# Seven products instead of eight in the down projections of an encoder's feed-forward layers

## The reference

```python
h = rms_norm(x, ffn_norm, NORM_EPS)
gate, up = jnp.split(h @ w_gate_up, 2, axis=-1)
return x + (jax.nn.silu(gate) * up) @ w_down
```

## Time and profile before

| what | value |
|---|---|
| median of 3 runs | 1811.87 us (1810.98 to 1812.22) |
| the profiled execution | 1812.14 us, of which its span is 1810.2 us |
| TensorE busy | 1759.2 us |
| VectorE busy | 1180.5 us |
| ScalarE busy | 798.6 us |
| GpSimd busy | 275.6 us |
| granted TensorE clock, mean | 0.994 of full |

### The profile page before, as it was taken

How to read it: one execution, slowest core, us unless ns; L and a number is a source line. 1 busy time by engine, 2 the same in 40 slices (tenths; PEclk the granted TensorE clock), 3 DMA queues, 4 the chain that set the end, 5 groups by cost and what they waited for, 6 DMA issues and landing times.

```text
span 1810.2 us, 28642 instructions
## 1 busy us (share of the span) xinstructions
PE 1759.2 (97%) x11280; PEld 1552.1 (86%) x11280; DVE 1180.5 (65%) x1955; ACT 798.6 (44%) x1772; POOL 275.6 (15%) x400
## 2 busy tenths in 40 slices
PE   6999999999999999999999999999899999999998
PEld 6888777778989898989888878777799898989896
DVE  5655888787656566666556468886877474747565
ACT  5233777644433333333332348775534242424242
POOL 3201436440000000000012015362400000000000
PEclk9999999999999999999999999999999999999999
DMA  5221000202222222221222210002122222212222
GB/s 173 62 67 47 25 2 25 71 1 82 71 70 70 70 70 71 68 72 48 69 70 59 59 36 26 2 25 71 35 71 70 70 70 64 69 61 67 67 81 82
DMA packets 121732, 108.20 MB, mean 60 GB/s; under 512 B 3360, under 2 KB 95648, under 8 KB 121600
## 3 DMA queue, kind: packets, MB, share of 16 engines
q1 hardware_dynamic: 120240, 101.79, 19.0%
q0 software_dynamic: 928, 3.02, 0.6%
q10 hardware_dynamic: 432, 1.57, 0.2%
HBM read 103.22 MB, written 3.15 MB: 59 GB/s over the span
## 4 chain that ended last, share of the span: by engine, by line
PE 89%; DVE 4%; ACT 2%; POOL 2%; issue 1%; DMA 0%; ACTq 0%; POOLq 0%
PE bank L1710 16%; PE bank L1712 14%; PE bank L1711 14%; PE bank L2032 12%; PE bank L2036 12%; PE bank L2034 12%; PE bank L1804 4%; PE bank L1795 3%; PE bank L1952 1%; DVE neg_max L1387 1%; PE bank L1751 1%; POOL hrstd L620 1%; PE bank L1790 1%; ACT stage L980 1%; PE bank L1728 1%
## 5 line engine op out<-in xcount | busy, mean ns | idle before, releaser
L1710 PE MATMUL bank<-w_hi,hT_hi 128*128 128x512 f32 (+1 forms) x624 | 245.5, 393 | 9.3 <-DVE x L1496 7.2
L1712 PE MATMUL bank<-w_hi,hT_lo 128*128 128x512 f32 (+1 forms) x624 | 234.4, 376 | 0.0
L1711 PE MATMUL bank<-w_lo,hT_hi 128*128 128x512 f32 (+1 forms) x624 | 233.8, 375 | 0.0
L618 POOL TENSOR_TENSOR ms<-ss,eps_col 128x1 f32<-128x1 f32 x30 | 6.2, 208 | 1052.9 <-ACT headsq L819 1052.9
L1281 DVE TENSOR_TENSOR x<-x,bank 128x512 f32<-128x512 f32 x120 | 81.3, 687 | 118.9 <-PE bank L1712 118.4
L1710 PEld LDWEIGHTS bank<-w_hi,hT_hi 128*128 128x128 f32 x624 | 118.0, 189 | 42.7 <-DVE x L1496 10.7
L1712 PEld LDWEIGHTS bank<-w_hi,hT_lo 128*128 128x128 f32 x624 | 118.0, 189 | 21.9
L1711 PEld LDWEIGHTS bank<-w_lo,hT_hi 128*128 128x128 f32 x624 | 118.4, 190 | 17.1
L2032 PE MATMUL bank<-hT_hi,w_hi 128*128 128x384 f32 x368 | 123.5, 336 | 0.7 <-issue 0.7
L2036 PE MATMUL bank<-hT_hi,w_lo 128*128 128x384 f32 x368 | 123.6, 336 | 0.0
L2034 PE MATMUL bank<-hT_lo,w_hi 128*128 128x384 f32 x368 | 123.3, 335 | 0.0
(11 more groups left out here) (214 smaller groups left out, 4610.4 us busy)
## 6 DMA issues: line engine op xcount, KB each, us to landing
x_raw<-in_w_gate_up_dram SPq DMA_DIRECT2D x44, 512.0 KB, 5.0
w_raw<-in_w_gate_up_dram SPq DMA_DIRECT2D x44, 512.0 KB, 4.0
w_raw<-in_w_in_dram SPq DMA_DIRECT2D x36, 512.0 KB, 3.7
w_raw<-in_w_down_dram SPq DMA_DIRECT2D x36, 512.0 KB, 3.8
w_raw<-in_w_out_dram SPq DMA_DIRECT2D x16, 512.0 KB, 3.7
x_raw<-in_w_down_dram SPq DMA_DIRECT2D x8, 512.0 KB, 3.7
out_dram<-stage SPq DMA_DIRECT2D x6, 512.0 KB, 2.6
gain<-in_gains_dram POOLq DMA_DIRECT2D x4, 512.0 KB, 4.1
```

Source lines behind the costliest of these rows:

```text
L1710: pe.matmul(out, a_hi, b_hi, start=first, stop=False)
L1711: pe.matmul(out, a_hi, b_lo, start=False, stop=False)
L1712: return pe.matmul(out, a_lo, b_hi, start=False, stop=last)
```

## The change

For the four middle groups of a layer (`SEVEN`), `down_seven(g)` takes the place of `down(g)`. The result of a group is seen as 2 x 2 blocks: two halves of the tokens (384 rows) by two halves of the columns (512); the inner dimension as two pairs of D_FF tiles. With A the activations and B the weights of the group:

| product | token part | weights | added to block of x |
|---|---|---|---|
| 0 | A11 | B11 | 11 |
| 1 | S1 = A21 + A22 | T1 = B12 - B11 | 22 |
| 2 | S2 = S1 - A11 | T2 = B22 - T1 | 12 (with product 0) |
| 3 | S4 = A12 - S2 | B22 | 12 (with product 1) |
| 4 | S3 = A11 - A21 | T3 = B22 - B12 | 22 (with 0 and 2) |
| 5 | A12 | B21 | 11 |
| 6 | A22 | T4 = B21 - T2 | 21 (with 0, 2 and 4) |

Each product is 2 inner tiles x 3 token tiles x 3 matmuls of 512 columns, and VectorE adds its three banks to x behind it. Even products use banks 6, 7 and 5, odd ones 2, 3 and 4. The token parts are split into halves in two places (`part_hi`, `part_lo`, 768 columns each), and the weights pass through the ring as before, 14 operands instead of 8. S1 and T1 to T4 (1024 columns each) are made by VectorE, the other token sums by GpSimd. B22 and B21 are loaded into the tile `gain` (a fifth raw buffer), B11 and B12 into the two w_raw. Tiles of these groups have no `act_high` and `act_low`; `gated` writes `act_raw` instead. In the tile that follows such a group the two w_raw buffers change places, and its first combinations are made two operands later.

The core of the diff, VectorE's list first:

```diff
@@ vector, stage of the next group's first tile @@
                     up_second(l, j - 1)
                     operand_low(l, s + 6)
+                    g = group_before(j)
+                    if g in SEVEN:
+                        operand_low(l, s + 7)
+                        operand_low(l, s + 8)
+                        down_combination(l, g, T1)
+                        gate_first(l, j)
+                        part_low(l, g, 0)
+                        operand_low(l, s + 9)
+                        operand_low(l, s + 10)
+                        down_combination(l, g, T2)
+                        up_first(l, j - 1)
+                        gated(l, j - 1)
+                        sum_first(l, g)
+                        operand_low(l, s + 11)
+                        part_low(l, g, 1)
+                        down_combination(l, g, T3)
+                        for i in range(12, 15):
+                            operand_low(l, s + i)
+                        for i in range(1, 6):
+                            add_seven(l, g, i - 1, 0)
+                            part_low(l, g, i + 1)
+                            add_seven(l, g, i - 1, 1)
+                            operand_low(l, s + (13 + 2 * i))
+                            add_seven(l, g, i - 1, 2)
+                            operand_low(l, s + (14 + 2 * i))
+                            if i == 2:
+                                down_combination(l, g, T4)
+                        for i in (5, 6):
+                            for m in range(3):
+                                add_seven(l, g, i, m)
+                        continue
@@ scalar @@
+                    if g in SEVEN:
+                        operand_high(l, s + 8)
+                        part_high(l, g, 0)
+                        silu_first(l, j)
+                        operand_high(l, s + 9)
+                        operand_high(l, s + 10)
+                        silu_second(l, j - 1)
+                        operand_high(l, s + 11)
+                        part_high(l, g, 1)
+                        for i in range(12, 15):
+                            operand_high(l, s + i)
+                        for i in range(1, 6):
+                            operand_high(l, s + (13 + 2 * i))
+                            part_high(l, g, i + 1)
+                            operand_high(l, s + (14 + 2 * i))
+                        operand_high(l, s + 25)
+                        continue
@@ gpsimd @@
+            def later_sum(l, g, n):
+                e = SEVEN.index(g)
+                if n == 0:
+                    pool.wait_ge(first_sum.sem, first_sum.at(l, e))
+                    out, a, b = act_quarter(1, 0), act_quarter(0, 0), act_quarter(1, 0)
+                elif n == 1:
+                    pool.wait_ge(part_lo_done.sem, part_lo_done.at(l, 7 * e))
+                    pool.wait_ge(later_sums.sem, later_sums.at(l, 3 * e))
+                    out, a, b = act_quarter(0, 0), act_sum[:, :, :], act_quarter(0, 0)
+                else:
+                    pool.wait_ge(part_lo_done.sem, part_lo_done.at(l, 7 * e + 1))
+                    pool.wait_ge(later_sums.sem, later_sums.at(l, 3 * e + 1))
+                    out, a, b = act_sum[:, :, :], act_quarter(0, 1), act_quarter(0, 0)
+                pool.tensor_tensor(out, a, b, ALU.subtract).then_inc(later_sums.sem, 1)
...
-                pool.wait_ge(h_ready.sem, h_ready.at(l, 2 * T - 1))
-
+                for g in SEVEN:
+                    later_sum(l, g, 0)
+                    later_sum(l, g, 1)
+                    later_sum(l, g, 2)
+
+                pool.wait_ge(ff_lo.sem, ff_lo.at(l, seven_operand(SEVEN[-1], 6, 1)))
                 pool.dma_start(gain[:, :],
@@ tensor @@
+                def down_seven(g):
+                    j = FIRST[g] + 3
+                    for i in range(7):
+                        pe.wait_ge(part_lo_done.sem, part_lo_done.at(l, 7 * SEVEN.index(g) + i))
+                        for k in range(2):
+                            r = seven_operand(g, i, k)
+                            b_hi, b_lo = ring_of(r)
+                            pe.wait_ge(ff_lo.sem, ff_lo.at(l, r))
+                            for m in range(3):
+                                b = (DOWN_W if i % 2 else DOWN_X)[m]
+                                if k == 0:
+                                    if i >= 2:
+                                        pe.wait_ge(x_added.sem, x_added.at(l, seven_added(g, i - 2, m)))
...
+                                pe.matmul(o, a_hi, b_hi, start=begin, stop=False, skip_group_check=True)
+                                pe.matmul(o, a_hi, b_lo, start=False, stop=False, skip_group_check=True)
+                                last = pe.matmul(o, a_lo, b_hi, start=False, stop=k == 1, skip_group_check=True)
@@ sync, load_seven @@
+                for b, kk, c in ((B22, 2, 1), (B11, 0, 0), (B12, 0, 1), (B21, 2, 0)):
...
+                    elif b == B11:
+                        sp.wait_ge(ff_lo.sem, ff_lo.at(l, operand(f0 + 3, 4)))
+                    elif b == B12:
+                        sp.wait_ge(ff_lo.sem, ff_lo.at(l, operand(f0 + 3, 3)))
+                    else:
+                        sp.wait_ge(ff_lo.sem, ff_lo.at(l, seven_operand(g, 3, 1)))
+                        sp.wait_ge(down_t.sem, down_t.at(l, 4 * SEVEN.index(g) + T3))
```

More of the change, by code:

```diff
@@ L69 @@
 GROUP = 4
+SEVEN = [_g for _g in range(LAST_G) if GROUPS[_g] == 4]
+PLAIN = [_j for _g in range(len(GROUPS)) if _g not in SEVEN for _j in range(FIRST[_g], FIRST[_g] + GROUPS[_g])]
+DOWN_X, DOWN_W = [6, 7, 5], [2, 3, 4]
+QUARTER = [(0, 0), (1, 1), (0, 1), (0, 1), (1, 1), (0, 0), (1, 0)]
+B11, B12, B22, B21 = range(4)
+T1, T2, T3, T4 = range(4)
 RING = 8
@@ L79, in group_before, with width @@
     return FIRST.index(j) - 1 if j and j in FIRST else None
+def width(g):
+    return 14 if g in SEVEN else 2 * GROUPS[g]
 def stage_start(j):
@@ L85, in stage_start @@
         return OUT_R
-    return OUT_R + 11 + 7 * (j - 2) + sum(2 * GROUPS[group_before(i)] for i in range(2, j) if group_before(i) is not None)
+    return OUT_R + 11 + 7 * (j - 2) + sum(width(group_before(i)) for i in range(2, j) if group_before(i) is not None)
 def operand(j, product):
@@ L113, in down_operand, with seven_operand, slots @@
     return first + c * n + k
-OPERANDS = OUT_R + 7 * FT + 2 * FT
+def seven_operand(g, i, k):
+    return stage_start(FIRST[g + 1]) + 7 + 2 * i + k
+def slots(j):
+    if j % 2 == 0:
+        return 2, 3
+    return (1, 0) if group_before(j - 1) in SEVEN else (0, 1)
+OPERANDS = OUT_R + 7 * FT + sum(width(_g) for _g in range(len(GROUPS)))
 PRODUCT_1 = [operand(_j, 1) for _j in range(FT)]
@@ L146, in down_slot @@
     return i % 2 + (2 if g == LAST_G else 0)
-LOADS = [[] for _ in range(4)]
+LOADS = [[] for _ in range(5)]
+DOWN_BUFFER = {B22: 4, B11: 0, B12: 1, B21: 4}
 for _j in range(FT):
-    LOADS[0 if _j % 2 else 2].append(("gate", _j))
-    LOADS[1 if _j % 2 else 3].append(("up", _j))
+    LOADS[slots(_j)[0]].append(("gate", _j))
+    LOADS[slots(_j)[1]].append(("up", _j))
     _g = LAST_G if _j == FT - 1 else group_before(_j)
-    if _g is not None:
+    if _g in SEVEN:
+        for _b in (B22, B11, B12, B21):
+            LOADS[DOWN_BUFFER[_b]].append(("down", _g, _b))
+    elif _g is not None:
         for _i in range(GROUPS[_g]):
@@ L160 @@
 for _j in range(FT):
-    _gs, _us = (0, 1) if _j % 2 else (2, 3)
+    _gs, _us = slots(_j)
     SOURCE[operand(_j, 1)] = (_gs, ("gate", _j), 0, None)
@@ L168 @@
     SOURCE[operand(_j, 3)] = (_us, ("up", _j), COLS, None)
+DOWN_MADE = {}
+for _g in SEVEN:
+    for _i, (_b, _t) in enumerate([(B11, None), (B11, T1), (B11, T2), (B22, None), (B12, T3), (B21, None), (B21, T4)]):
+        for _k in range(2):
+            _r = seven_operand(_g, _i, _k)
+            SOURCE[_r] = (DOWN_BUFFER[_b], ("down", _g, _b), _k * COLS, None)
+            if _t is not None:
+                DOWN_MADE[_r] = 4 * SEVEN.index(_g) + _t
 for _g, _n in enumerate(GROUPS):
     for _c in range(2):
-        for _k in range(_n):
+        for _k in range(0 if _g in SEVEN else _n):
             _i = _c * _n // 2 + _k // 2
@@ L179 @@
 for _r in range(down_operand(LAST_G, 0, 0)):
-    _last = any(_r == down_operand(_g, _c, _n - 1) for _g, _n in enumerate(GROUPS) for _c in range(2))
-    USED_AT.append((USED_AT[-1] if USED_AT else 0) + (T if _last else 0 if _r == OUT_R - 1 else 1))
+    _last = any(_r == down_operand(_g, _c, _n - 1) for _g, _n in enumerate(GROUPS) if _g not in SEVEN for _c in range(2))
+    _seven = any(_r == seven_operand(_g, _i, 1) for _g in SEVEN for _i in range(7))
+    USED_AT.append((USED_AT[-1] if USED_AT else 0) + (T if _last else 3 if _seven else 0 if _r == OUT_R - 1 else 1))
+ADDED_AT = [4 * T + sum(21 if _h in SEVEN else 2 * T for _h in range(_g)) for _g in range(len(GROUPS) + 1)]
+FIRST_AT = {PRODUCT_1[_j] + (2 if group_before(_j - 1) in SEVEN else 0): _j for _j in range(2, FT)}
 LAST_USED = [(0, 3), (1, 1)]
```

(16 more changed lines are left out.)

163 lines of the change are left out of this document (133 added, 30 removed).

## The result

| | median us | range | ratio to before |
|---|---|---|---|
| before | 1811.92 | 1810.98 to 1812.22 | |
| after | 1843.01 | 1842.15 to 1843.35 | 1.0172 (95% interval 1.0160 to 1.0184) |

A forecast was written before the change was run, and what follows sets the result against it. TensorE set the pace before; the change fills VectorE, so a group takes 36.9 us, 3.65 more than 33.3. 8 x 3.65 + 0.85 = 30.0 us on 1812.14 gives 1842 us, range 1810 to 1858.

The forecast's parts named there:

- TensorE's saving, 4.16 us per group: Down projection: 126 matmuls per inner pass where there were 144, 18 x 0.231 us less, leaving 29.1 us.
- VectorE's steps, 43.5 us over stage and group: All VectorE instructions from the stage ahead to the group's end, 43.5 us against 43.7 us of TensorE.
- The turns with GpSimd, 4.85 us per group: GpSimd's three sums block VectorE's low half of part 1, third combination and operand 12: 4.85 us, at most 5.5.
- The loop starts at 11.0 us: VectorE's loop over products 2 to 6 begins 11.0 us after the down projection starts, behind operands 12 to 14.
- Turn 2 waits 0.9 us for the block: In the loop's second turn, the block loaded behind operand 14 and two ScalarE high halves come 0.9 us late.
- The next tile's combinations, 3.1 us in turn 5: VectorE makes two pairs of gate and up combinations for the next tile in the loop's fifth turn: 3.1 us.
- The unit of 0.60 us: Distance between starts of VectorE instructions of 512 columns when nothing is waited for, used to price its steps.
- TensorE's stall, 7.8 us: Per group: 0.5 + 3.75 us at products 1 and 2, the rest in pieces at later products and the next tile's first.
- First group of the first layer, 0.85 more: That group had its second block late before the change, so 0.85 us was added there once.
- The clock: Part of the slower-still rival: stalls lower TensorE's granted clock, or GpSimd goes before operand 11; +6 to +7 us per group, 0.08.
- The free-turns rival: GpSimd's sums cost VectorE nothing, so the loop starts at 6.15 and a group lasts 32.1 us: 1803 us, chance 0.09.

The follow-up runs named there:

- the kernel with the high half of part 2 ahead of operand 15: Against the kernel with VectorE's list rearranged and all sums on VectorE, ScalarE makes part 2's high half before operand 15: 1785.04 us.
- the filled run: The changed kernel with 14 more matmuls of 512 columns in product 1 of each group, where TensorE would stand idle ahead of product 2: 1841.94 us.
- the run with late combinations: The changed kernel with the next tile's combinations moved behind the adds of product 5 and ScalarE's keep step moved along: 1833.43 us.
- the new order with GpSimd's sums: The changed kernel with VectorE's and ScalarE's lists rearranged, the three later sums still on GpSimd and operand 15 ahead of part 2 on ScalarE: 1822.14 us.
- the run with 4-column sums: The changed kernel with GpSimd's three sums per group cut to 4 of their 768 columns: 1806.09 us.

## Why the prediction was right

It gave 1842 us and a group of 36.95 us; measured were 1843.0 and 37.11. Step by step:

- **TensorE's saving, 4.16 us per group.** Held: without a gap a group lasts 29.6 us (the kernel with the high half of part 2 ahead of operand 15), 0.5 over the 29.1 worked out.
- **VectorE's steps, 43.5 us over stage and group.** From operand 4 to the last add of the group VectorE is busy for 47.2 us:

```profile
597.78:650.24 52.46, 47.56 (x215) 39.59 (x214) 47.21 (x64) 19.39 (x33) 7.26 (x3) 0.97 0.16 51
```

Of these, 4.5 are the waits for GpSimd inside three steps (2.16 + 2.86 + 2.33 - 0.95 - 1.23 - 0.68). That leaves 42.7, and the last of the 22 low halves (0.6) stands behind the stretch: 43.3. Held.
- **The turns with GpSimd, 4.85 us per group.** The three waits are 4.5 us, and cutting the sums gave 37.11 - 32.5 = 4.6 us. Held. Each sum took 1.7 us of its own, not 1.83.
- **The loop starts at 11.0 us.** It started at 621.48 - 610.84 = 10.64. Operand 11, part 1, the third combination and operands 12 to 14 stand in the worked-out order.
- **Turn 2 waits 0.9 us for the block.** It waited 0.65; with its other steps the turn is 0.1 under.
- **The next tile's combinations, 3.1 us in turn 5.** They took 2.8. The unit of 0.60 us and the 0.1 for a wait on VectorE's own result give 2.6 to 2.8, so 3.1 was a slip of at least 0.3 in the sum. (By the same units the four combinations of the group come to 5.0, not 5.1.)
- **A step that was missed:** operand 19 is made from the fourth combination and stands ahead of part 4 on ScalarE; VectorE waits 0.89 us for it, and turn 3 is 0.97 longer. I had followed ScalarE's list for the block of turn 2 and not for that.
- **The errors** are -0.36, -0.1, +0.97 and -0.3; they make +0.2 together. That the end came out within 0.2 us per group is luck: one wait of nearly 1 us was missing, and three terms were too large by 0.8 together.
- **TensorE's stall, 7.8 us.** It lost 8.0 (37.11 - 29.1). Of these 4.9 are idle stretches (37.11 - 32.21 busy), with 0.28 ahead of product 1 where I had 0.5 and 3.27 ahead of product 2 where I had 3.75. The rest lies in matmuls that took longer, those at half clock among them, which I didn't have in the forecast.
- **First group of the first layer, 0.85 more:** it didn't come. That group lasted 37.2 us, within the 36.99 to 37.22 of the eight, and VectorE's wait in its turn 2 was 0.76 us. Eight groups at 37.1 instead of 36.95, 1.2 us together, made up for it, which is luck too.
- **The clock.** Held to be a rival at +6 us per group together with other things. It did fall, in all eight groups, and it cost the kernel about nothing: the filled run, without any fall in its groups, is 1.1 us faster, which its executions hardly tell from none, and the one group without a fall in the run with late combinations is as long as the others. TensorE wasn't what the group waited for. Where it is, a fall of the same length costs 1.5 us (34.13 against 32.64 in the new order with GpSimd's sums).
- **The free-turns rival** said 1803 for a kernel without any turn lost; the run with 4-column sums gave 1806.

## What to carry to other kernels

A change that cuts the work of the engine that sets the pace has to be priced by the list of every engine that feeds it. Here VectorE is busy for 21 us more per group (11.36 + 35.03 against 9.15 + 16.18), of which 4.5 are waits for GpSimd. That ate the 4 us saved on TensorE, and only ordering the steps by when TensorE needs each gave the saving back. In a list written by hand, look for each wait on a late result and ask what stands behind it that is wanted earlier: moving one line of ScalarE's list was worth 13 us. Sums of two SBUF tensors on GpSimd are not free beside a full VectorE: they held it up for most of their own length.

## What the runs showed of the hardware

- The turns between VectorE and GpSimd were expected. New is how exact they are: in each of the eight groups after the change GpSimd's three sums last 2.24, 2.37 and 2.65 us to within 0.01, and VectorE's blocked steps of 512, 768 and 1024 columns end some 0.55, 0.82 and 1.08 us after GpSimd's, 0.13 to 0.15 us less than their own length (0.68, 0.95, 1.23).
- TensorE's granted clock fell to 1.2 GHz for 3.4 us in each of the eight groups after the change, behind 3.2 to 3.3 us of idling ahead of product 2. The same gap in the run with late combinations brought it in seven groups of eight, and a gap of 3.0 to 3.1 us in the new order with GpSimd's sums in seven of eight, for 3.4 or 6.8 us. With the sums on VectorE in the same places the gap there is 1.4 to 1.7 us, and no group has a fall; with the gap filled there is none either. At half clock matmuls of 512 columns start 0.43 us apart instead of 0.23.
- What a fall costs depends on who sets the pace behind it. Where it was TensorE, one of 3.4 us cost 1.5 us (34.13 against 32.64) and one of 6.8 us cost 2.8 (35.43). Where it was VectorE, eight of them made 1.1 us together (1843.0 against 1841.9), which the executions hardly tell from nothing.
